# Differential attention in turn: bank pairs that change roles each unit, score halves interleaved, one scaling of the weights, low parts and squares on POOL

## The reference, cut to what matters

```python
def one_block(qb):                     # 128 queries, 4 heads; c = 0, 1 are the two halves of a head (64 wide)
    s = jnp.einsum('bhqcd,bhkcd->bhcqk', qb, k_all).astype(jnp.float32) * (DIFF_DH ** -0.5)
    p = jax.nn.softmax(s, axis=-1)     # 768 keys
    a = (p[:, :, 0] - lam.astype(jnp.float32) * p[:, :, 1]).astype(v_all.dtype)
    return jnp.einsum('bhqk,bhkd->bhqd', a, v_all)

def diff_merge(o, norm_g, lam_init):
    return merge_heads(rmsnorm(o, norm_g) * (1.0 - lam_init))

def rmsnorm(x, g):
    y = xf * lax.rsqrt(jnp.mean(xf * xf, axis=-1, keepdims=True) + EPS)
    return (y * g.astype(jnp.float32)).astype(x.dtype)
...
mix = jnp.concatenate([gla_merge(og, r, gla_norm_g[l]), diff_merge(od, diff_norm_g[l], lam_init)], axis=-1) @ w_out[l]
```

## Time and profile before

| | us |
|---|---|
| median of 3 runs (1596.98 to 1597.98) | 1597.84 |
| the profiled execution, its own time | 1597.36 |
| its span, first to last instruction | 1595.5 |

### The profile page before, as it was taken

The page is one execution under the profiler, slowest core; times in us unless marked ns, Lnnn a source line. Parts: engine busy times, 40 slices in busy tenths (PEclk is TensorE's granted clock), DMA queues, the critical chain, the costliest instruction groups (busy, mean ns, idle before and its releaser), DMA issues.

```text
span 1595.5 us, 19834 instructions
## 1 busy us (share of the span) xinstructions
PE 1549.6 (97%) x7939; PEld 1251.3 (78%) x7939; DVE 930.7 (58%) x1405; ACT 732.9 (46%) x1158; POOL 120.5 (8%) x89
## 2 busy tenths in 40 slices
PE   8999998989999999999999899999989999999998
PEld 5777876778788888888878677788778888888887
DVE  4866878876644433334646545365757785267745
ACT  5463545874432222323443767455556553244432
POOL 0000214630000000000100111130010000000000
PEclk9999999999999999999999999999999999999999
DMA  9721112005333233223231222143213232333221
GB/s 376 268 103 54 53 54 88 19 8 191 119 132 120 82 118 103 93 68 103 85 116 60 74 72 67 41 145 93 91 43 103 73 114 78 107 106 104 77 89 61
DMA packets 49841, 157.70 MB, mean 99 GB/s; under 512 B 5683, under 2 KB 12467, under 8 KB 49493
## 3 DMA queue, kind: packets, MB, share of 16 engines
q1 hardware_dynamic: 48352, 151.80, 29.2%
q10 hardware_dynamic: 1396, 4.63, 0.8%
HBM read 154.31 MB, written 2.10 MB: 98 GB/s over the span
## 4 chain that ended last, share of the span: by engine, by line
PE 78%; DVE 11%; ACT 8%; issue 2%; POOL 0%; DMA 0%; DVEq 0%; SPq 0%; ACTq 0%
PE pall L2331 18%; PE pall L2333 18%; PE pall L2332 18%; PE pall L2891 2%; PE pall L2365 2%; PE pall L2367 2%; PE pall L2366 2%; PE pall L2893 2%; PE pall L2892 2%; DVE wlo L1350 1%; ACT whi L590 1%; ACT e L908 1%; DVE statd L1725 1%; DVE W L1361 1%; DVE R L1363 1%
## 5 line engine op out<-in xcount | busy, mean ns | idle before, releaser
L1350 DVE TENSOR_TENSOR wlo<-raw,whi 128x1024 fp32r<-128x1024 f32 (+2 forms) x263 | 294.3, 1119 | 290.0 <-ACT whi L590 289.9
L590 ACT ACTIVATE whi<-raw 128x1024 fp32r<-128x1024 f32 (+2 forms) x263 | 247.0, 941 | 178.5 <-PE pall L2333 164.6
L2331 PE MATMUL pall<-h5h,whi 128*128 128x512 f32 x320 | 124.9, 390 | 1.0 <-DVE wlo L1350 1.0
L2332 PE MATMUL pall<-h5l,whi 128*128 128x512 f32 x320 | 124.5, 389 | 0.0
L2333 PE MATMUL pall<-h5h,wlo 128*128 128x512 f32 x320 | 124.5, 389 | 0.0
L2331 PE MATMUL pall<-h2h,whi 128*128 128x512 f32 x320 | 124.5, 389 | 0.0
L2332 PE MATMUL pall<-h2l,whi 128*128 128x512 f32 x320 | 124.5, 389 | 0.0
L2333 PE MATMUL pall<-h2h,wlo 128*128 128x512 f32 x320 | 124.5, 389 | 0.0
L2331 PEld LDWEIGHTS pall<-h5h,whi 128*128 128x128 f32 x320 | 60.1, 188 | 14.1 <-DVE wlo L1350 1.4
L2333 PEld LDWEIGHTS pall<-h5h,wlo 128*128 128x128 f32 x320 | 60.1, 188 | 12.6
L2332 PEld LDWEIGHTS pall<-h2l,whi 128*128 128x128 f32 x320 | 60.1, 188 | 12.6
(11 more groups left out here) (519 smaller groups left out, 3679.7 us busy)
## 6 DMA issues: line engine op xcount, KB each, us to landing
raw<-in_weights SPq DMA_DIRECT2D x204, 512.0 KB, 3.5
mraw<-in_wmod SPq DMA_DIRECT2D x32, 512.0 KB, 5.0
mod<-in_weights SPq DMA_DIRECT2D x16, 512.0 KB, 14.6
raw<-in_weights SPq DMA_DIRECT2D x25, 256.0 KB, 2.6
raw<-in_weights SPq DMA_DIRECT2D x32, 192.0 KB, 2.3
xT<-in_x SPq DMA_DIRECT2D x4, 512.0 KB, 5.8
xT<-in_x ACTq DMA_DIRECT2D x1, 2048.0 KB, 7.6
out_y<-xT SPq DMA_DIRECT2D x5, 256.0 KB, 2.3
```

The costliest lines, as they stand in the source:

```text
L590: e.activation(whi[j % 3][:, 0:cols(j)], raw[j % 4][:, 0:cols(j)], ACT.Copy).then_inc(s.hi, 1)
L1350: e.tensor_tensor(wlo[j % 3][:, 0:n], raw[j % 4][:, 0:n], f(whi[j % 3][:, 0:n]), ALU.subtract).then_inc(s.lo_v, 1)
L2331: e.matmul(o_, a[:, kk, :], xh(k), start=(k == 0), stop=False)
L2332: e.matmul(o_, a[:, kk, :], xl(k), start=False, stop=False)
```

## The change

Eight edits, all in this stage:

1. **Bank pairs.** `pair(what, n)` replaces `dpair`: c = 1 of unit n takes the pair that the turned weights of unit n-3 leave, c = 0 of unit n the pair that c = 1 of unit n-1 leaves, and turn(n-2) the pair that c = 0 of unit n-1 leaves.
2. **Order of the scores.** The 256-column products of c = 1 come first, then the 512-column products of both halves in turn, then the 256-column products of c = 0. `fill` of the pair of c = 0 stands ahead of the products in turn, so that it holds up the 512-column products of c = 1 as well.
3. **PE's step** is scores(n), turn(n-2), values(n-3): one unit earlier than before, and the turn behind the scores.
4. **Weights.** Only e1 is scaled: e0 + e1 · (-lambda · sum0 / sum1), with a ratio on DVE (`diff_ratio`, one column), so that the weights are p0 - lambda · p1 times sum0, and POOL's scaling of e1 is gone. The output's norm takes that factor out again: its epsilon becomes eps · sum0 squared for each query (`es`, one column on POOL), which PE adds to the sum of squares as ones times a diagonal array DG (`head_eps`), a second product with ones for each head.
5. **Squares** of heads 0 to 2 go from ACT to POOL (`head_square`).
6. **Low parts** Kl, Ql of heads 1 to 3 and mixl of heads 0 to 2 go from DVE to POOL (`key_low`, `query_low`, `head_low`).
7. **Head steps** stand earlier: ACT's copy at step 6, 10, 14 (was 7, 11, 15), its root at 7, 11, 15 (was 8, 12, 16), DVE's newton at 8, 12, 16 (was 9, 13, 17), its scaling one step behind; head copies of odd heads go to tmp[2].
8. The scales 1/8 and 1 - lambda_init go into two gain vectors (two DVE instructions of one column, early in the program); two of the other attention's four splits move from steps 1 and 4 to 12 and 13; `mix_out` takes banks 4, 5, 2, 3, 0, 1.

PE's part of the diff, with the pairs; `freed` says what `fill` waits for:

```diff
+        def pair(what, n):
+            return 2 * (0, 2, 1)[(n - 1 if what == 0 else n) % 3]
+
+        wo_bank = (4, 5, 2, 3, 0, 1, 4, 5)
...
+            def scores(n):
...
+                b1, b0 = pair(1, n), pair(0, n)
+                fill(b1)
+                fill(b1 + 1)
+                w.wait_ge(s.kql, 2 * h + 2)
+                for k in range(3):
+                    product(1, k, 512, 768)
+                fill(b0)
+                fill(b0 + 1)
+                for k in range(3):
+                    mm = product(1, k, 0, 512)
+                    if k == 2:
+                        mm.then_inc(s.sc, 1)
+                    product(0, k, 0, 512)
+                for k in range(3):
+                    mm = product(0, k, 512, 768)
+                mm.then_inc(s.sc, 1)
+                for c, b in ((1, b1), (0, b0)):
+                    freed[b] = freed[b + 1] = [(s.mx, 2 * n + 2 - c), (s.ex, 2 * n + 2 - c)]
...
+            def head_sums(h):
+                b = 6 + h % 2
+                w.wait_ge(s.dev, h + 1)
+                w.wait_ge(s.dgd, h + 1)
+                e.matmul(bank(b), ones[:, :], DG[:, :], start=True, stop=False)
+                w.wait_ge(s.dsq, h + 1)
+                e.matmul(bank(b), ones[:, :], tmp[1][:, :], start=False, stop=True).then_inc(s.p_sum, 1)
...
+            for n in range(19):
                 if n == 3:
                     query_sums(3)
...
+                    scores(n)
...
+                if 0 <= n - 2 < 16:
+                    turn_weights(n - 2)
+                if 0 <= n - 3:
+                    values(n - 3)
+                if n in (7, 11, 15):
+                    head_sums((n - 7) // 4)
+            mix_out(0, 0)
+            head_sums(3)
```

ACT's loop (each step: copy, two exponentials, then what the step has besides):

```diff
+            for n in range(18):
+                if n >= 2:
+                    i = n - 2
+                    w.wait_ge(s.tp, i + 1)
+                    w.wait_ge(s.pv, i - 2)
+                    e.activation(PT[i % 3][:, :, :], win(bank(pair("turn", i), 768)), ACT.Copy).then_inc(s.ta, 1)
...
+                if n in (2, 3, 12, 13):
+                    mix_gla((2, 3, 12, 13).index(n))
...
+                if n in (10, 14):
+                    head_high((n - 10) // 4)
+                if n in (6, 10, 14):
+                    head_copy((n - 6) // 4)
+                if n in (7, 11, 15):
```

DVE's loop, and POOL's:

```diff
+            for n in range(17):
+                if n >= 1:
+                    diff_ratio(n - 1)
                 if n < 16:
                     diff_max(n, 1)
                     diff_max(n, 0)
-                    diff_recip(n, 1)
...
+                if n >= 1:
+                    diff_weights(n - 1)
                 if n < 16:
-                    diff_recip(n, 0)
+                    diff_recip(n)
```

```diff
             for n in range(16):
-                col = 8 * (n % 4) + 4
-                e1 = EB[n % 3][1][:, :]
-                w.wait_ge(s.drec, 2 * n + 1)
-                e.tensor_scalar(e1, e1, sd[:, col + 3:col + 4], nlam, ALU.mult, ALU.mult).then_inc(s.dnl, 1)
+                c = 8 * (n % 4) + 2
+                w.wait_ge(s.ex, 2 * n + 2)
+                e.tensor_scalar(es[:, n:n + 1], sd[:, c:c + 1], sd[:, c:c + 1], EPS * 128, ALU.mult, ALU.mult).then_inc(s.des, 1)
+                if n in (0, 4):
+                    key_low(n // 4 + 1)
+                if n in (1, 5, 9):
+                    query_low((n - 1) // 4 + 1)
...
+                if n in (5, 9, 13):
+                    head_eps((n - 5) // 4)
+                if n in (10, 14):
+                    head_low((n - 10) // 4)
+                if n in (6, 10, 14):
+                    head_square((n - 6) // 4)
```

More of the change, by code:

```diff
@@ L494, in build @@
         HS = (3, 3, 3, 6)
-        diff_units = [(i, i // 4, i % 4) for i in range(16)]
         fox_units = [(i, 2 * (i // 8) + i % 2, (0, 3, 1, 2)[i // 2 % 4]) for i in range(32)]
@@ new lines, in turn_weights, with values @@
+            def turn_weights(i):
+                b = pair("turn", i)
+                fill(b)
+                fill(b + 1)
+                w.wait_ge(s.dw, i + 1)
+                for k in range(6):
+                    c = slice(128 * k, 128 * k + 128)
+                    t = e.transpose(bank(b, 768)[:, c], EB[i % 3][0][:, c], ident[:, :])
+                t.then_inc(s.tp, 1)
+                freed[b] = freed[b + 1] = [(s.ta, i + 1)]
+            def values(i):
+                h, qt = i // 4, i % 4
+                b = 6 + h % 2
+                qs = slice(128 * qt, 128 * qt + 128)
+                if qt == 0:
+                    fill(b)
+                w.wait_ge(s.ta, i + 1)
+                w.wait_ge(s.vg, 6 + 6)
+                for k in range(6):
+                    mm = e.matmul(bank(b)[:, qs], Vd[:, k, 128 * h:128 * h + 128], PT[i % 3][:, k, :],
+                                  start=(k == 0), stop=(k == 5))
+                mm.then_inc(s.pv, 1)
```

233 lines of the change are left out of this document (106 added, 127 removed).

## The result

| | us |
|---|---|
| kernel before, median of 4 runs (1596.98 to 1597.98) | 1597.62 |
| changed kernel, median of 4 runs (1585.38 to 1588.08) | 1586.88 |
| ratio, with its 95% interval | 0.9932 (0.992 to 0.9943) |
| profiled execution of the changed kernel | 1585.89 |

A forecast was written before the change was run, and what follows sets the result against it. PE, 97% busy, was the bound. 290.3 + 12 x 4.10 + 1.2 + 1.7 + 1.7 + 0.2 + 11.6, then 0.85, gave 356.75 against 361.14: 4.4 less, so 1593.4 us, range 1589.5 to 1600.5.

The forecast's parts named there:

- The stretch up to unit 2 keeps its work and its waits.: Start of the attention stage: nothing changes there, so unit 2's last score product stays at 287.38.
- unit 3's R: R is the moment a unit's bank pair of c = 0 is free; for unit 3 it was put at 290.3.
- More gain: Rival: the 13.5 us half-clock stretch ends sooner, or the unit comes out at 4.05; 1590 us, chance 0.12.
- the loop PE, ACT, PE: Each unit: scores and transposes, ACT's copy and exponential, then PE again at the next R, 4.05 us later.
- The 0.05 for two loops that pass on each other's delays: Each unit: 0.05 us added because loops of 4.00 and 4.05 pass on delays, making the unit 4.10.
- The late copy behind dq3's root: After unit 3's exponentials: a root and a split on ACT make the copy 1.2 us late.
- A head step: Steps 7 and 11: a head's sums on PE, two products with ones of 0.85 each, add 1.7 us per step.
- The 0.2 for POOL's square: Steps 11 and 15: POOL's square may come late for PE, taken as 0.2 us at each.
- The end: From unit 15's R to the first mix product: 11.6 us, with the root setting it.
- the halves overlap: Score products: the rival denied this overlap, 0.69 us more per unit, 9.0 us in all, 1602.4 us; chance 0.08.
- the rival had 3.6: Second product with ones: POOL's square 2.0 us late at steps 11 and 15, 0.4 becomes 4.0, 1597.0 us; chance 0.10.
- The rival of the clock: Attention stage: frequent PE stops bring one or two more half-clock stretches, costing 1.5 to 3 us, about 1595.7; chance 0.10.

The follow-up runs named there:

- one_sum: The changed kernel without the first of each head's two products with ones, so without the epsilon of those four norms: 1585.50 us, ratio 0.9924.
- onr_nopool: The changed kernel with bank roles, step order and places, weights as before, and POOL's low parts and squares back on DVE and ACT: 1594.04 us, ratio 0.9979.

## Why the prediction was wrong

The step that failed is "The stretch up to unit 2 keeps its work and its waits." It put unit 3's R at 290.3; it was 286.81 (first 512-column product of c = 0), 3.5 of the 7.1 us by which the profiled execution (1585.89) lies below the 1593.0 forecast for it. The chain behind unit 2's last score product was as forecast, 3.10 against 2.94; that product came at 283.71 and not at 287.38:

```profile
283.71 0.28 PE L2776 MATMUL pall<-Kh,Ql 64*128 64x256 f32 x1
...
286.81 0.49 PE L2776 MATMUL pall<-Kh,Qh 64*128 64x512 f32 x2 [0.36 <-ACT e L920]
```

PE's products up to there were the same. A split of ACT and DVE's Kl had gone, but these had not held up unit 2, whose maxima waited for PE before (timeline of DVE):

```profile
287.13 1.82 DVE L1725 TENSOR_REDUCE statd<-pall 128x1 f32<-128x768 f32 x2 [1.38 <-PE pall L2744]
```

The waits were not the same, and with them moved the stretch at half clock: before, 7.9 us of it lay behind 279, where PE sets the pace; in the changed kernel's profile none, in its second profile 3.4. The kernel one_sum is the same program up to unit 3; in its profile 7.4 us lay behind 279, and its R was at 289.51, so 2.7 of the 3.5 go with the place of the stretch alone.

```profile
289.51 0.50 PE L2776 MATMUL pall<-Kh,Qh 64*128 64x512 f32 x2 [0.36 <-ACT e L920]
```

In the table "0 to 3" follows that column: 11.1 to 11.3 us in all kernels with 0, 11.8 to 12.4 with 3.4, 12.9 to 14.3 with 6 to 8.2. The rival "More gain" named this way, but gave it 3.4 us in all and a chance of 0.12. Why the clock falls in one place or the next stays open: the order of the first score products moved it, and so did nothing at all, from run to run.

The unit was right in each step. From R = 337.89: last product R + 1.06 (1.11 forecast), transposes' end R + 2.14 (2.20), copy R + 2.18 (2.23), exponential R + 2.88 (2.92). So the loop PE, ACT, PE sets the unit, with 4.00 where 4.05 was forecast: PE takes up R 0.14 behind ACT's read of the sum, as the earlier trace rows had it. PE's own work is shorter than the 4.00 that stood beside the loop. Its third product of 256 columns begins 0.26 ahead of R, and 0.12 ahead of the next product where the pair has long been free (unit 8); so it stands 0.14 or so in each unit, and its own work is about 3.86, an estimate from these rows (units 15 and 8):

```profile
337.55 0.20 ACT L920 ACTIVATION_READ_ACCUMULATOR e<-pall,statd 128x1 f32 x1
337.63 0.28 PE L2776 MATMUL pall<-Kh,Ql 64*128 64x256 f32 x1
337.89 0.50 PE L2776 MATMUL pall<-Kh,Qh 64*128 64x512 f32 x2
```
```profile
309.13 0.27 PE L2776 MATMUL pall<-Kh,Ql 64*128 64x256 f32 x1
...
309.25 0.39 PE L2776 MATMUL pall<-Kh,Qh 64*128 64x512 f32 x1
```

The 0.05 for two loops that pass on each other's delays was not needed, and 4.10 was 4.00: 0.1 in each of twelve units, 1.2 us.

The other terms were mis-sized in the same direction. The late copy behind dq3's root cost 0.9 (1.2 forecast). A head step cost 1.12 and not 1.7, since behind it both halves' products begin together. The 0.2 for POOL's square was nothing: the two products with ones stand 0.86 apart at every head (341.21 and 342.07), as at head 3, whose square is ACT's (351.64 and 352.50). The end took 10.9 and not 11.6; the root did not set it alone, since without it there 7.4 us remained of 8.0. Together 1.2 + 0.3 + 1.2 + 0.2 + 0.7 = 3.6, and with the start 7.1. Head 3's second product cost its 0.86.

The gain of the units, 8.2 us, had more than one parent, and the prediction gave all of it to the new loop. Going from before to after by runs: 3.4 us with head steps on two buffers and the split one step later, in turn and all that is left (59.3 to 55.9; the kernel before had 3.4 us of half clock there as well), 2.7 with POOL's work, 0.5 with the weights, 1.6 with the roles, the order and the places. Taken back singly from the changed kernel, they are worth 0.3 (POOL), 0.8 (in turn), 1.1 (weights) and 1.6 (roles): with the new roles the maxima have room (ACT waits for none between 287 and 349), and DVE's extras no longer reach PE. The first 3.4 us were not taken apart by runs, but unit by unit the traces of before and of onr_nopool agree within 0.05 us up to unit 10. Behind it 1.4 lie in the step where ACT waited 2.19 us ahead of head 0's split, 1.2 in that of head 1's, and 0.9 in the steps between, where the clock stood at half; the splits of that run wait nowhere. At the end the same sequence of kernels takes 10.0, 10.6, 12.7, 12.0 and 8.0 us: POOL's work, which helps in the units, made PE wait there until the roles were new. The 3.9 us of the last step hold that wait; against the kernels without it (10.0 and 10.6) the shorter pipeline is worth some 2.0 to 2.6.

The rivals: the halves overlap (329.89, "x2"), and even out of turn they did. In the changed kernel PE's products waited nowhere for POOL's square, where the rival had 3.6. The rival of the clock had the sign wrong: from 287 to 349 it is 1.00 throughout, in spite of pairs that change roles each unit, so the swing that the Trainium skill ("TensorE: Matmul & The Clock Gate", section A second HAM failure mode: psum-queue depth-cycling) describes did not show here; the windows leave PE 0.8 us of idle time in 51.

## What to carry to other kernels

Before costing a stretch at half clock, find which engine sets the pace in it: 6.8 us cost 0.1 under DVE, and 6.0 cost 2.3 where PE was the last to finish, and a change that merely moves waits can move such a stretch from one side to the other. Where a loop waits at several engines in turn, the parts of a change overlap: undo each singly and each looks small. And count what stands behind the last exponential: a pipeline one step shorter pays there once, here 2.0 us (10.0 to 8.0), and work moved to another engine can take back there what it gave in the loop (2.1 of 2.7 us with the old roles).

## What the runs showed that was not expected

- Products of 64 rows start out of program order. With all of c = 1 ahead of all of c = 0, c = 0's product of 512 columns began beside c = 1's last ones of 512 (333.65 and 333.69), so the order in the code decided little (units of 3.97 and 4.00 us).
- Filling one wait of PE with unused products moved the fall of the clock 6 us further (from 272.2 to 278.2) and the median was 2.1 us longer; filling all three kept it at 1.00 from the start to 1582 in the profiled run.
- A DVE operation of 0.69 us on 128x512 took 1.04 and 1.44 us while POOL worked (L1371 at 269.19, 272.79 and 275.32), and these stand on the path to the first maximum.
